# A diffusion step on one core: first modulation in four rounds, and low halves moved between engines

## The chip, the cores and the metric

The kernel runs on one core of one Trainium2 chip. The metric is the device time of the program in microseconds. Three runs of the kernel before took 1401.58, 1401.72 and 1401.97 us, median 1401.72. The program is bound by its order on one core; there is no traffic between cores.

## The reference

One inference step of a backbone with one trunk layer, for 128 context and 512 latent tokens of width 1024 (640 tokens in all, every weight shared, each kind of token with its own modulation vectors). Cut to what matters here:

```python
def trunk_layer(x, cond, ...):
    mod = (jax.nn.silu(cond) @ w_mod + b_mod)[:, None, :]          # 1024 -> 9 * 1024
    sh1, sc1, g1, sh2, sc2, g2, sh3, sc3, g3 = jnp.split(mod, N_MOD, axis=-1)
    h = rms_norm(x, norm_pre[0]) * (1.0 + sc1) + sh1
    x = x + 0.5 * g1 * rms_norm(swiglu(h, ffn_w_in[0], ffn_w_out[0]), norm_post[0])
    h = rms_norm(x, norm_pre[1]) * (1.0 + sc2) + sh2
    m, s_f, s_b = mixer(h, ...)                                    # Fourier mixing and HGRN2 scans
    x = x + g2 * rms_norm(m, norm_post[1])
    h = rms_norm(x, norm_pre[2]) * (1.0 + sc3) + sh3
    x = x + 0.5 * g3 * rms_norm(swiglu(h, ffn_w_in[1], ffn_w_out[1]), norm_post[2])
```

`swiglu(h, w_in, w_out)` is `(silu(h @ w_in[:, :2816]) * (h @ w_in[:, 2816:])) @ w_out`. Everything is float32.

## The kernel before, in words

**Precision.** Every large product is made of three TensorE passes over rounded operands: a float32 matrix is split into a high half (rounded to the fp32r format by ScalarE) and a low half (full minus high, by GpSimd or VectorE), and the passes are high x high, high x low, low x high. A slab is one block of weights (1024 x 128, 512 KB). Its life is: load (the queue of SyncE), high half on ScalarE (`next_hi`, L1211), low half on GpSimd in two instructions of 512 columns (`subtract`, L541) or on VectorE in one (`slab_low`, L1838, for the slabs listed in `LO_DVE`), and then the matmuls, after which `slab_done` frees its buffer.

**The order** is written out by hand, one list for each engine, with semaphores between them. `plan()` says for each slab which buffer it uses and after which slab it may be loaded.

**The start.** The tokens are normalized and transposed to features (XH). The first shift and scale vectors are `silu(cond)` times four blocks of 512 columns of `w_mod` (blocks 0 and 2 hold the first half of the features' shift and scale, 1 and 3 the second). `early_mod(i)` makes one block: 8 matmuls of 32 output rows (traced as 16, since float32 takes two instructions), four beside each other in the array. ScalarE copies the result (`mod_rows`, L1254), `fold_mod` (L685) turns it round into columns, VectorE adds the bias and forms the gains (L1745, L1755), then for each feature tile k the affine (`first_affine`, L1762, two instructions), ScalarE's high half (`first_hi`, L1258) and VectorE's low half (L1777). TensorE is kept busy by `keep_busy` in between. `first_slab(n, ks)` (L877) multiplies slab n with the feature tiles ks. The first three slabs are interleaved with the second round of the modulation; the low halves of slabs 1 and 2 on GpSimd wait until VectorE has finished tile 1 and tile 4 (`h0_ready`).

**The FFN's input product.** Of its 22 pairs of slabs (gate and value), three are made plainly; for the other 19 four blocks of the product are made with seven block products instead of eight (`seven_products`, L813 is `product`). They need combinations of the tokens (T1, T2, T4 as high and low halves, T3) and sums of weight blocks (S). `token_lows` has GpSimd make the low halves of T2, T1 and T4 in a row, 128 x 1280 each (L550); `seven_low` then makes those of each pair. The first product of the first pair writes the first bank of its set, the second the second bank, and so on.

**The FFN's output product** is `out0A` (token tiles 0 to 2) and then `out0B` (tiles 3 and 4), 22 slabs each, L630 to L632.

## Time and profile before

| | |
|---|---|
| median of three runs | 1401.72 us |
| the profiled execution | 1401.38 us |
| its span | 1399.2 us |
| TensorE matmul busy | 1376.1 us (98%) |
| VectorE busy | 745.8 us (53%) |
| ScalarE busy | 582.2 us (42%) |
| GpSimd busy | 727.0 us (52%) |
| granted TensorE clock, mean | 0.999 |
| DMA | 173.34 MB, mean 124 GB/s |

The span runs from the first to the last instruction; the profiled execution's time is 2.2 us longer. A granted clock of 1.00 is 2.4 GHz, 0.50 is 1.2 GHz. In the rows PE is TensorE's matmul, PEld its weight load, DVE VectorE, ACT ScalarE, POOL GpSimd. Matmuls are pipelined, so one matmul's duration is longer than the distance to the next.

### The profile page before, as it was taken

Reading aid. Unit: us, or ns where it says so; the run is one execution under the profiler, and the core shown is the slowest. Engines: PE = TensorE matmul, PEld = TensorE weight load, DVE = VectorE, ACT = ScalarE, POOL = GpSimd, SP = SyncE. Lnnn points to the kernel's source line nnn. Section 1 sums busy time; section 2 is a strip of 40 time slices with the busy share of each in tenths; the row PEclk is TensorE's granted clock in tenths of the full one; section 3 lists DMA queues with packets and bytes.
Section 4 is the critical chain, followed back from the end, with each engine's and each line's share of the span. In section 5 each row is a group of like instructions: output and inputs, shape, how many; then the busy total and the mean of one; then the engine's idle time right before and its main releaser. Section 6 shows DMA issues by size and latency. Waiting matters only on the chain.

```text
span 1399.2 us, 23472 instructions
## 1 busy us (share of the span) xinstructions
PE 1376.1 (98%) x9537; PEld 1258.3 (90%) x9537; DVE 745.8 (53%) x1109; ACT 582.2 (42%) x946; POOL 727.0 (52%) x530
## 2 busy tenths in 40 slices
PE   6999999999999999999999999999999999999998
PEld 5789898999887888999999999988999999998886
DVE  5686555766702421478776312135877666676033
ACT  5243333334534663244445222257344443455243
POOL 1475546465966672323223433542576555667663
PEclk9999999999999999999999999999999999999999
DMA  9756676233535651212112222333122223334465
GB/s 346 260 160 217 214 237 210 62 92 90 176 124 166 194 174 49 61 55 62 53 41 66 76 76 76 103 109 91 46 76 81 78 84 91 91 105 152 135 194 181
DMA packets 215294, 173.34 MB, mean 124 GB/s; under 512 B 6472, under 2 KB 175636, under 8 KB 215060
## 3 DMA queue, kind: packets, MB, share of 16 engines
q1 hardware_dynamic: 212448, 170.61, 39.0%
q8 instruction: 76, 1.25, 0.4%
q10 hardware_dynamic: 2740, 1.24, 0.3%
q14 instruction: 30, 0.25, 0.1%
HBM read 168.65 MB, written 3.17 MB: 123 GB/s over the span
## 4 chain that ended last, share of the span: by engine, by line
PE 89%; DVE 4%; DMA 2%; ACT 2%; POOL 2%; issue 1%; SPq 0%; DVEq 0%; ACTq 0%
PE PP L813 33%; PE PP L611 22%; PE PP L630 8%; PE PP L632 8%; PE PP L631 8%; PE PP L669 2%; DMA W_in<-in_ffn_w_in 1%; PE PP L877 1%; PE PP L655 1%; PE PP L1003 1%; POOL W_lo L541 1%; PE PP L1019 1%; POOL T_lo L550 0%; DVE XTOK L1802 0%; PE PP L1073 0%
## 5 line engine op out<-in xcount | busy, mean ns | idle before, releaser
L541 POOL TENSOR_TENSOR W_lo<-W_in,W_hi 128x512 fp32r<-128x512 f32 (+1 forms) x304 | 382.3, 1283 | 443.5 <-ACT W_hi L1211 436.1
L550 POOL TENSOR_TENSOR W_lo<-W_in,W_hi 128x512 fp32r<-128x512 f32 x112 | 176.3, 1587 | 185.1 <-ACT S_hi L1438 182.0
L1211 ACT ACTIVATE W_hi<-W_in 128x1024 fp32r<-128x1024 f32 x143 | 150.9, 1056 | 226.0 <-PE PP L632 115.8
L630 PE MATMUL PP<-W_hi,Mlo 128*128 128x512 f32 x440 | 172.0, 391 | 1.3 <-POOL W_lo L541 0.9
L632 PE MATMUL PP<-W_hi,Mhi 128*128 128x512 f32 x440 | 171.2, 389 | 0.0
L631 PE MATMUL PP<-W_lo,Mlo 128*128 128x512 f32 x440 | 171.2, 389 | 0.0
L611 PE MATMUL PP<-Hhi,W_hi 128*128 128x320 f32 (+2 forms) x608 | 146.6, 316 | 0.0
L813 PE MATMUL PP<-Hhi,W_hi 128*128 128x320 f32 x452 | 141.3, 313 | 1.3 <-POOL W_lo L550 0.9
L611 PE MATMUL PP<-Hlo,W_hi 128*128 128x320 f32 (+2 forms) x608 | 142.3, 309 | 0.0
L611 PE MATMUL PP<-Hhi,W_lo 128*128 128x320 f32 (+2 forms) x608 | 142.3, 309 | 0.0
L813 PE MATMUL PP<-Hhi,W_lo 128*128 128x320 f32 x452 | 139.6, 309 | 0.0
L813 PE MATMUL PP<-Hlo,W_hi 128*128 128x320 f32 x452 | 139.6, 309 | 0.0
L550 POOL TENSOR_TENSOR S_lo<-S_in,S_hi 128x512 fp32r<-128x512 f32 x76 | 116.4, 1531 | 0.0
L611 PEld LDWEIGHTS PP<-Hhi,W_hi 128*128 128x128 f32 x608 | 101.3, 188 | 3.9 <-issue 2.7
L611 PEld LDWEIGHTS PP<-Hhi,W_lo 128*128 128x128 f32 x608 | 102.7, 188 | 0.0
L611 PEld LDWEIGHTS PP<-Hlo,W_hi 128*128 128x128 f32 x608 | 102.7, 188 | 0.0
L630 PEld LDWEIGHTS PP<-W_hi,Mlo 128*128 128x128 f32 x440 | 82.6, 188 | 20.0 <-POOL W_lo L541 1.7
L632 PEld LDWEIGHTS PP<-W_hi,Mhi 128*128 128x128 f32 x440 | 82.6, 188 | 17.2
L631 PEld LDWEIGHTS PP<-W_lo,Mlo 128*128 128x128 f32 x440 | 82.6, 188 | 16.9
L813 PEld LDWEIGHTS PP<-Hhi,W_hi 128*128 128x128 f32 x452 | 84.8, 188 | 11.8 <-issue 9.1
L813 PE MATMUL PP<-T_hi,S_hi 128*128 128x320 f32 x304 | 94.0, 309 | 0.8 <-DVE M L2035 0.8
L813 PE MATMUL PP<-T_hi,S_lo 128*128 128x320 f32 x304 | 93.9, 309 | 0.0
(297 smaller groups left out, 3002.3 us busy)
## 6 DMA issues: line engine op xcount, KB each, us to landing
W_in<-in_ffn_w_out SPq DMA_DIRECT2D x176, 256.0 KB, 3.2
W_in<-in_ffn_w_in SPq DMA_DIRECT2D x84, 512.0 KB, 4.5
modl<-in_w_mod SPq DMA_DIRECT2D x14, 2048.0 KB, 7.9
W_in<-in_w_in SPq DMA_DIRECT2D x32, 512.0 KB, 3.8
modw<-in_w_mod SPq DMA_DIRECT2D x4, 2048.0 KB, 14.3
HL<-g_rows SPq DMA_DIRECT2D x6, 512.0 KB, 6.2
V_in<-in_w_in SPq DMA_DIRECT2D x10, 256.0 KB, 3.7
O_in<-in_w_out SPq DMA_DIRECT2D x10, 256.0 KB, 5.4
```

The lines of the kernel that those rows point to most:

```text
L541: return nc.gpsimd.tensor_tensor(lo[:, k0:k1, :], full[:, k0:k1, :], hi[:, k0:k1, :].bitcast(fp32), ALU.subtract)
L550: return nc.gpsimd.tensor_tensor(lo, full, hi.bitcast(fp32), ALU.subtract)
L611: m = mm(out[:, 0:c1 - c0], w[:, k, :], src[:, c0:c1], start=lead and n == 0 and a == 0, stop=tail and n == len(x) - 1 and a == 2)
L630: mm(out, xh, wh, start=lead and kk == 0, stop=False)
L631: mm(out, xh, wl, start=False, stop=False)
L632: m = mm(out, xl, wh, start=False, stop=tail and kk == 1)
L655: return nc.tensor.transpose(out, in_, ident[0:k, 0:k])
L669: m = mm(PP[3][32 * q:32 * q + 32, 0, :], S2[:, k, 30 - 2 * i:62 - 2 * i], w[:, k, :], start=first and k < 4, stop=k >= 4, skip_group_chec ...
L813: m = mm(out, wk[:, k, :], xk[:, k, :], start=not add and k == 0 and a == 0, stop=k == KH - 1 and a == 2, skip_group_check=add)
L877: m = mm(PP[n][:, half, 0:HALF], w[:, k, :], src[:, half * HALF:(half + 1) * HALF], start=k == 0 and a == 0, stop=k == KT - 1 and a == 2)
L1003: m = mm(near(pair_of(hd, lev))[32 * q:32 * q + 32, ch, :], KX[lev % 2][:, at:at + 32], queries, start=True, stop=True)
L1211: A(W[i][0], W[i][2], ACT.Copy).then_inc(hi_done, 1)
```

## The change

Four things are changed.

1. The first modulation is made in four rounds of 256 features (two tiles k) instead of two of 512. Each round loads 256 columns of the shift and 256 of the scale (`modw`, now eight buffers of 1 MB), makes them with matmuls of 256 columns, copies 256 columns and turns them with two matmuls instead of four. Loads, TensorE, ScalarE and VectorE are ordered by these rounds: slabs 0 and 1 are loaded behind the first round, slab 2 behind the second. ScalarE rounds slabs 0 and 1 before it copies the first row. `keep_busy` runs 32 times instead of 30.
2. GpSimd's low half of slab 2 waits for feature tile 2 instead of tile 4.
3. In both FFNs GpSimd's low half of T4 is made behind the low half of the first gate's slab. In the first pair of the first FFN the banks are 4, 5, 0, 3 instead of 4, 2, 0, 3, and the wait for the last of the three plain pairs stands before the third product instead of the second; the second pair gets two waits for the banks it shares.
4. In `out0B` VectorE makes the low half of slab 2 and GpSimd that of slab 3, instead of the other way round.

On TensorE, from the token transposes on, in the kernel before. `modw_162` to `modw_165` are the four blocks of 512 columns, `modw_164` to `modw_171` of the changed kernel the eight of 256; L669 and L679 are `mod_slab`, L685 and L696 `fold_mod`, L655 and L665 transposes, L877 and L895 `first_slab`.

```order
L655 MATMUL PP<-ident,YB 128x128 x40
L669 MATMUL PP<-modw_162,S_169 32x512 x8
L669 MATMUL PP<-modw_163,S_169 32x512 x8
L685 MATMUL PP<-ident,modrow_160 128x32 x4
L655 MATMUL PP<-ident 128x128 x30
L877 MATMUL PP<-Hhi,W_hi 128x320 x2
```

The same place in the changed kernel:

```order
L665 MATMUL PP<-ident,YB 128x128 x40
L679 MATMUL PP<-modw_164,S_175 32x256 x8
L679 MATMUL PP<-modw_165,S_175 32x256 x8
L696 MATMUL PP<-ident,modrow_160 128x32 x2
L665 MATMUL PP<-ident 128x128 x32
L895 MATMUL PP<-Hhi,W_hi 128x320 x2
L895 MATMUL PP<-Hlo,W_hi 128x320 x2
L895 MATMUL PP<-Hhi,W_lo 128x320 x2
L895 MATMUL PP<-Hhi,W_hi 128x320 x2
L895 MATMUL PP<-Hlo,W_hi 128x320 x2
L895 MATMUL PP<-Hhi,W_lo 128x320 x2
L679 MATMUL PP<-modw_166,S_175 32x256 x8
```

The second round's matmuls now stand behind two pieces of the first slabs, where eight pieces stood before the second round of 512 columns; the third and fourth follow between later pieces.

On GpSimd, where the seven-product stage of the first FFN begins, in the kernel before. W12 is the first gate's slab, W2 the first value's, S0 and S2 are sums of weight blocks.

```order
L550 TENSOR_TENSOR T2_lo_213<-T2_in_214,T2_hi_212 128x1280
L550 TENSOR_TENSOR T1_lo_216<-T1_in_217,T1_hi_215 128x1280
L550 TENSOR_TENSOR T4_lo_219<-T4_in_220,T4_hi_218 128x1280
L550 TENSOR_TENSOR W12_lo_141<-W12_in_142,W12_hi_140 128x512
L550 TENSOR_TENSOR S_lo0_144<-S_in0_145,S_hi0_143 128x512
```

The same place in the changed kernel:

```order
L557 TENSOR_TENSOR T2_lo_219<-T2_in_220,T2_hi_218 128x1280
L557 TENSOR_TENSOR T1_lo_222<-T1_in_223,T1_hi_221 128x1280
L557 TENSOR_TENSOR W12_lo_141<-W12_in_142,W12_hi_140 128x512
L557 TENSOR_TENSOR T4_lo_225<-T4_in_226,T4_hi_224 128x1280
L557 TENSOR_TENSOR S_lo0_144<-S_in0_145,S_hi0_143 128x512
```

The low half of T4 has gone behind that of the first gate. The diff, without line numbers' shifts, the placement of the new buffers and renamed counts:

```diff
--- before.py
+++ after.py
@@ -135,7 +136,7 @@
     BASE, BUF, FREE, ORDER, NEED, FRESH = plan()
 
     FIRST_LO = [(0, 0), (1, 0), (2, 0), (0, 1), (1, 1), (2, 1)]
-    LO_DVE = [BASE["out0B"] + m for m in (3, 7, 10, 13, 17)]
+    LO_DVE = [BASE["out0B"] + m for m in (2, 7, 10, 13, 17)]
     LO_DVE += [BASE["out1B"] + m for m in (3, 6, 9, 12, 15, 18, 20, 21)]
 
     top = [(nc.sbuf_base + 31) // 32 * 32]
...
@@ -380,6 +381,8 @@
 
     def seven_banks(f, p):
 
+        if (f, p) == (0, 0):
+            return [bank(n)[:, 0:HALF] for n in (4, 5, 0, 3)]
         sets = (((4, 2, 0, 3), (5, 2, 1, 3)), ((4, 5, 0, 1), (6, 7, 2, 3)))[f]
         return [bank(n)[:, 0:HALF] for n in sets[p % 2]]
 
...
@@ -407,8 +410,8 @@
 
         wm = w_mod[0].rearrange("(k p) n -> p k n", p=P)
         def load_early_mod(i):
-            n = MOD_ROUNDS[i // 2][i % 2]
-            sp.dma_start(modw[i][:, :, :], wm[:, :, n * 512:(n + 1) * 512]).then_inc(sem(f"modw_in{i}"), 16)
+            first_col = i % 2 * D + i // 2 * 256
+            sp.dma_start(modw[i][:, :, :], wm[:, :, first_col:first_col + 256]).then_inc(sem(f"modw_in{i}"), 16)
 
         def load(i, k0, kn, src):
 
...
@@ -460,17 +463,21 @@
 
         load_early_mod(0)
         load_early_mod(1)
-        for n in range(3):
-            load_in0(n)
+        load_in0(0)
+        load_in0(1)
         load_early_mod(2)
         load_early_mod(3)
+        load_in0(2)
+        for i in range(4, 7):
+            load_early_mod(i)
+        load_early_mod(7)
         load_in0(3)
         load_mod(0)
-        sp.wait_ge(sem("mod_mm"), MOD_EARLY)
+        sp.wait_ge(sem("mod_mm"), MOD_FIRST)
         load_mod(1)
         def next_mod(i):
 
-            sp.wait_ge(sem("mod_mm"), MOD_EARLY + (1 if i == 2 else i))
+            sp.wait_ge(sem("mod_mm"), MOD_FIRST + (1 if i == 2 else i))
             load_mod(i)
 
         for n in (4, 5):
...
@@ -544,13 +551,13 @@
         for i, half in FIRST_LO:
             pool.wait_ge(hi_done, i + 1)
             if half == 0 and i:
-                pool.wait_ge(sem("h0_ready"), (1, KT // 2)[i - 1])
+                pool.wait_ge(sem("h0_ready"), (1, 2)[i - 1])
             subtract(i, 4 * half, 4 * half + 4).then_inc(sem("first_lo"), 1)
         def low(hi, lo, full):
             return nc.gpsimd.tensor_tensor(lo, full, hi.bitcast(fp32), ALU.subtract)
 
         def token_lows(f):
-            for n, x in enumerate((T2, T1, T4)):
+            for n, x in enumerate((T2, T1)):
                 pool.wait_ge(sem("t_hi"), 3 * f + n + 1)
                 low(*(y[:, :, :] for y in x)).then_inc(sem("t_lo"), 1)
 
...
@@ -562,6 +569,9 @@
             pool.wait_ge(sem("s_made"), 4 * p + 3)
             pool.wait_ge(sem("seven_hi"), 7 * p + 1)
             low(*(x[:, 0:KH, :] for x in gate)).then_inc(sem("seven_lo"), 1)
+            if p == f * SEVEN:
+                pool.wait_ge(sem("t_hi"), 3 * f + 3)
+                low(*(y[:, :, :] for y in T4)).then_inc(sem("t_lo"), 1)
             pool.wait_ge(sem("seven_hi"), 7 * p + 4)
             low(*(x[:, :, :] for x in s1)).then_inc(sem("seven_lo"), 1)
             pool.wait_ge(sem("seven_hi"), 7 * p + 5)
...
@@ -661,27 +671,28 @@
         transpose(PP[2][:, 1, 0:36], rowsB[:, :]).then_inc(sem("vec_T"), 1)
         pe.wait_ge(sem("ones_set"), 2)
 
-        def mod_slab(w, i, first=False):
+        def mod_slab(w, i, first=False, cols=slice(0, 512)):
 
 
             for k in range(KT):
                 q = k % 4
-                m = mm(PP[3][32 * q:32 * q + 32, 0, :], S2[:, k, 30 - 2 * i:62 - 2 * i], w[:, k, :],
+                m = mm(PP[3][32 * q:32 * q + 32, 0, cols], S2[:, k, 30 - 2 * i:62 - 2 * i], w[:, k, :],
                        start=first and k < 4, stop=k >= 4, skip_group_check=not first)
             m.then_inc(sem("mod_mm"), 1)
 
         def early_mod(i):
             pe.wait_ge(sem(f"modw_in{i}"), 16)
             pe.wait_ge(sem("silu_c"), 2)
-            if i == 2:
-                pe.wait_ge(sem("modrow"), 1)
-            mod_slab(modw[i], i % 2, i % 2 == 0)
-
-        def fold_mod(i, rows):
+            r = i // 2
+            if r > 1:
+                pe.wait_ge(sem("modrow"), r - 1)
+            mod_slab(modw[i], i % 2, i % 2 == 0, slice(r % 2 * 256, r % 2 * 256 + 256))
+
+        def fold_mod(i, rows, first_at):
 
             pe.wait_ge(sem("modrow"), i + 1)
-            for q in range(4):
-                at = i * P + q * 32
+            for q in range(rows.shape[1] // P):
+                at = first_at + q * 32
                 m = mm(PP[3][:, 1, at:at + 32], rows[:, q * P:(q + 1) * P], ident[:, P:P + 32],
                        start=True, stop=True)
             m.then_inc(sem("mod_fold"), 1)
...
@@ -709,9 +720,9 @@
             first_tile(t)
         early_mod(0)
         early_mod(1)
-        fold_mod(0, modrow[0])
+        fold_mod(0, modrow[0], 0)
         pe.wait_ge(sem("x0_feat"), NCH)
-        keep_busy(30, PP[2][:, 1, 0:P])
+        keep_busy(32, PP[2][:, 1, 0:P])
 
 
         def to_features(b, t):
...
@@ -832,19 +843,26 @@
             pe.wait_ge(sem("seven_lo"), 5 * p + 1)
             if second and f:
                 pe.wait_ge(sem("hid_ready"), 3 * EARLY_PAIRS)
+            elif second:
+                pe.wait_ge(sem("u3_done"), 1)
             elif not first and not second:
                 pe.wait_ge(sem("hid_a"), p - 1)
             product(x, quadrant(gate, 0, KH), b11).then_inc(sem("product"), 1)
             pe.wait_ge(sem("seven_lo_dve"), 2 * p + 1)
             if first:
                 pe.wait_ge(sem("t_lo"), 3 * f + 1)
-                pe.wait_ge(sem("hid_ready"), (1 + f) * EARLY_PAIRS)
-            elif not (f and second):
+                if f:
+                    pe.wait_ge(sem("hid_ready"), 2 * EARLY_PAIRS)
+            elif second and not f:
+
+                pe.wait_ge(sem("hid_ready"), EARLY_PAIRS)
+            elif not second:
                 pe.wait_ge(sem("u3_done"), back)
             product(y, s2, T2).then_inc(sem("product"), 1)
             pe.wait_ge(sem("seven_lo"), 5 * p + 2)
             if first:
                 pe.wait_ge(sem("t_lo"), 3 * f + 2)
+                pe.wait_ge(sem("hid_ready"), (1 + f) * EARLY_PAIRS)
             elif not second:
                 pe.wait_ge(sem("hid_b"), p - 1)
             product(z, s1, T1).then_inc(sem("product"), 1)
...
@@ -893,16 +911,31 @@
             if n in MOD_AFTER:
                 late_mod(MOD_AFTER.index(n))
 
-        for k in range(KT // 2):
+        first_slab(0, (0,))
+        first_slab(1, (0,))
+        early_mod(2)
+        early_mod(3)
+        first_slab(0, (1,))
+        fold_mod(1, modrow[1], 64)
+        first_slab(1, (1,))
+        first_slab(2, (0, 1))
+        for k in (2, 3):
             first_slab(0, (k,))
             first_slab(1, (k,))
-        early_mod(2)
-        early_mod(3)
-        first_slab(2, (0,))
-        fold_mod(1, modrow[1])
-        first_slab(2, (1, 2, 3))
-        for n in range(3):
-            first_slab(n, range(KT // 2, KT))
+        early_mod(4)
+        early_mod(5)
+        first_slab(2, (2,))
+        fold_mod(2, modrow[2], 128)
+        first_slab(2, (3,))
+        early_mod(6)
+        early_mod(7)
+        first_slab(0, (4,))
+        fold_mod(3, modrow[3], 192)
+        first_slab(0, (5,))
+        first_slab(1, (4, 5))
+        first_slab(0, (6, 7))
+        first_slab(1, (6, 7))
+        first_slab(2, range(KT // 2, KT))
         late_mods(2)
         for j in range(1, EARLY_PAIRS):
             if j == 1:
...
@@ -1249,25 +1282,32 @@
         act.wait_ge(sem("lb_max"), 1)
         A(LB[:, 1:3, :], LB[:, 1:3, :], ACT.Exp).then_inc(sem("lb_exp"), 1)
 
-        def mod_rows(slabs, rows):
+        def mod_rows(slabs, rows, cols):
             act.wait_ge(sem("mod_mm"), slabs)
-            A(rows[:, :], PP[3][:, 0, :], ACT.Copy).then_inc(sem("modrow"), 1)
+            A(rows[:, :], PP[3][:, 0, cols], ACT.Copy).then_inc(sem("modrow"), 1)
+
+        def first_rows(r):
+            mod_rows(2 * r + 2, modrow[r], slice(r % 2 * 256, r % 2 * 256 + 256))
 
         def first_hi(k):
             act.wait_ge(sem("h0_32"), k + 1)
             A(Hhi[:, k, :], HL32[:, k, :], ACT.Copy).then_inc(sem("h0_hi"), 1)
 
         next_hi()
-        mod_rows(2, modrow[0])
         next_hi()
+        first_rows(0)
         first_hi(0)
         first_hi(1)
         next_hi()
+        first_rows(1)
         first_hi(2)
         first_hi(3)
-        mod_rows(MOD_EARLY, modrow[1])
-        for k in range(KT // 2, KT):
-            first_hi(k)
+        first_rows(2)
+        first_hi(4)
+        first_hi(5)
+        first_rows(3)
+        first_hi(6)
+        first_hi(7)
         next_hi()
 
 
...
@@ -1763,11 +1803,22 @@
                                     MV[:, k, cnd:cnd + 1], ALU.mult, ALU.add)
             m.then_inc(sem("h0_32"), 1)
 
+        def first_vectors(r):
+
+            def groups(ap):
+                step = ap.ap[1][0]
+                return bass.AP(ap.tensor, ap.offset, [ap.ap[0], [KT * step, 2], [step, 2]])
+
+            span = slice(2 * r, 2 * KT)
+            for cnd in range(2):
+                sums = PP[3][:, 1, 64 * r:64 * r + 64].rearrange("p (q i c) -> p i q c", q=2, c=2)
+                link(V.tensor_tensor(groups(MV[:, span, cnd]), sums[:, 0:2, :, cnd], groups(VA[:, span]), ALU.add))
+
         dve.wait_ge(sem("x0_feat"), NCH)
-        for r in range(2):
+        for r in range(ROUNDS):
             dve.wait_ge(sem("mod_fold"), r + 1)
-            mod_vectors(r * P, MOD_ROUNDS[r])
-            ks = range(r * KT // 2, (r + 1) * KT // 2)
+            first_vectors(r)
+            ks = range(2 * r, 2 * r + 2)
             gains(0, True, False, ks[0], ks[-1] + 1)
             first_affine(ks[0])
             for k in ks:
...
@@ -1841,7 +1892,7 @@
 
             for t in GROUP[0]:
                 y_gain(b, t, 0)
-            slab_low(OUT_B[b], 3)
+            slab_low(OUT_B[b], 3 if b else 2)
             for t in GROUP[0]:
                 y_gain(b, t, 1)
             if b == 0:
```

## Rows read from the trace of the kernel before

**Rows 1.** The page, part 1: busy time of TensorE, share of the span, instructions.

```profile
PE 1376.1 (98%) x9537; PEld 1258.3 (90%) x9537; DVE 745.8 (53%) x1109; ACT 582.2 (42%) x946; POOL 727.0 (52%) x530
```

**Rows 2.** TensorE's waits: who waited for whom: us, times, longest.

```profile
PE PP L877 <- DVE Hlo L1777: 1.3, 3, 0.7
PE PP L630 <- POOL W_lo L541: 0.9, 1, 0.9
PE PP L813 <- POOL W_lo L550: 0.9, 1, 0.9
PE PP L813 <- DVE M L2035: 0.8, 1, 0.8
```

**Rows 3.** Timeline of TensorE: start, duration, instructions merged [idle before them <- releaser].

```profile
21.32 1.92 PE L669 MATMUL PP<-modw,S 128*32 128x512 f32 x16 [0.71 <-DMA modw<-in_w_mod]
24.71 1.08 PE L685 MATMUL PP<-ident,modrow 128*128 128x32 f32 x8 [1.46 <-ACT modrow L1254]
25.62 5.14 PE L655 MATMUL PP<-ident 128*128 128x128 f32 x30
30.52 0.54 PE L877 MATMUL PP<-Hhi,W_hi 128*128 128x320 f32 x2
...
37.72 3.64 PE L669 MATMUL PP<-modw,S 128*32 128x512 f32 x32
...
42.28 0.97 PE L685 MATMUL PP<-ident,modrow 128*128 128x32 f32 x8
...
46.67 0.53 PE L877 MATMUL PP<-Hhi,W_hi 128*128 128x320 f32 x2 [0.70 <-DVE Hlo L1777]
...
58.49 1.92 PE L669 MATMUL PP<-modl,S 128*32 128x512 f32 x16
```

**Rows 4.** Stretches: length, busy time of each engine, granted clock, DMA share, GB/s.

```profile
14.00:16.00 2.00, 2.00 (x21) 2.00 (x20) 0.81 (x1) 1.98 (x3) 0.00 (x0) 1.00 1.06 389
...
22.00:23.00 1.00, 1.00 (x12) 0.13 (x4) 0.00 (x0) 0.00 (x0) 0.00 (x0) 1.00 1.20 290
...
28.00:29.00 1.00, 1.00 (x6) 1.00 (x5) 0.91 (x2) 1.00 (x3) 0.00 (x0) 0.50 1.06 391
```

**Rows 5.** Timelines of ScalarE, VectorE and GpSimd in the start.

```profile
24.08 0.58 ACT L1254 ACTIVATE modrow<-PP 128x512 f32<-128x512 f32 x1
...
29.05 1.79 DVE L1762 TENSOR_SCALAR HL<-XH,Avec,MV 128x128 f32<-128x128 f32 x2
...
46.44 0.80 DVE L1762 TENSOR_SCALAR HL<-XH,Avec,MV 128x128 f32<-128x128 f32 x2
...
29.28 1.28 POOL L541 TENSOR_TENSOR W_lo<-W_in,W_hi 128x512 fp32r<-128x512 f32 x1 [3.76 <-DVE Hlo L1777]
```

**Rows 6.** Timeline of TensorE's weight loads within one modulation block.

```profile
19.14 0.13 PEld L669 LDWEIGHTS PP<-modw,S 128*32 128x32 f32 x4 [0.30 <-issue]
```

**Rows 7.** Timelines of TensorE, VectorE, GpSimd at the first seven-product stage.

```profile
88.36 0.39 PE L813 MATMUL PP<-T_hi,S_hi 128*128 128x320 f32 x1 [0.79 <-DVE M L2035]
...
76.75 3.34 DVE L1929 TENSOR_TENSOR S_in<-S_in,W_in 128x512 f32<-128x512 f32 x1
...
73.19 9.73 POOL L550 TENSOR_TENSOR T_lo<-T_in,T_hi 128x1280 fp32r<-128x1280 f32 x3 [7.19 <-ACT T_hi L1450]
```

**Rows 8.** Timelines of TensorE, VectorE, ScalarE, GpSimd at the third slab of out0B.

```profile
441.55 0.50 PE L630 MATMUL PP<-W_hi,Mlo 128*128 128x512 f32 x1 [0.93 <-POOL W_lo L541]
...
439.13 1.23 DVE L1838 TENSOR_TENSOR W_lo<-W_in,W_hi 128x1024 fp32r<-128x1024 f32 x1 [44.81 <-ACT W_hi L1211]
...
436.83 2.27 ACT L1211 ACTIVATE W_hi<-W_in 128x1024 fp32r<-128x1024 f32 x2 [6.82 <-DMA W_in<-in_ffn_w_out]
...
437.97 3.52 POOL L541 TENSOR_TENSOR W_lo<-W_in,W_hi 128x512 fp32r<-128x512 f32 x2 [4.75 <-ACT W_hi L1211]
```

**Rows 9.** Timelines of VectorE and GpSimd at the second seven-product stage.

```profile
1001.57 3.45 DVE L1930 TENSOR_TENSOR I_in<-W_in,I_in 128x512 f32<-128x512 f32 x1
...
997.89 9.95 POOL L550 TENSOR_TENSOR T_lo<-T_in,T_hi 128x1280 fp32r<-128x1280 f32 x3 [13.97 <-ACT T_hi L1450]
1007.80 1.72 POOL L550 TENSOR_TENSOR W_lo<-W_in,W_hi 128x512 fp32r<-128x512 f32 x1
```

More of the change, by code:

```diff
@@ L61 @@
 ]
-MOD_ROUNDS = ((0, 2), (1, 3))
+ROUNDS = 4
+MOD_FIRST = 2 * ROUNDS
 MOD_AFTER = [2, 3, 5]
@@ L225, in hybrid_step_kernel @@
     rowsB = place("rowsB", [36, P], fp32, at=tile_at(8) + 512)
-    modrow = [place(f"modrow{r}", [P, 512], fp32, at=tile_at(8) + 1024 + 2048 * r) for r in range(2)]
+    modrow = [place(f"modrow{r}", [P, 256], fp32, at=tile_at(8) + 1024 + 1024 * r) for r in range(ROUNDS)]
     late_at = [tile_at(MOD_LATE_FREE), tile_at(FT + MOD_LATE_FREE)]
     early_at = late_at[0] + 16384 + 2 * 2048
-    modw = [place(f"modw{s}", [P, KT, 512], fp32, at=at)
-            for s, at in enumerate((h_at + KT * TB, early_at, early_at + 16384, early_at + 2 * 16384))]
+    modw = [place(f"modw{s}", [P, KT, 256], fp32, at=at + s % 2 * 8192) for s, at in enumerate(
+        at for at in (h_at + KT * TB, early_at, early_at + 16384, early_at + 2 * 16384) for _ in range(2))]
     modl = [place(f"modl{s}", [P, KT, 512], fp32, at=late_at[s]) for s in (0, 1)]
@@ L480, in _ @@
         load(BASE["in0s"] + 1, 0, KT, w0[:, :, DFF + j * P:DFF + (j + 1) * P])
-        sp.wait_ge(sem("mod_mm"), MOD_EARLY + 2)
+        sp.wait_ge(sem("mod_mm"), MOD_FIRST + 2)
         load(BASE["in0s"], 0, KT, w0[:, :, j * P:(j + 1) * P])
@@ L887, in late_mod @@
             if i == 0:
-                pe.wait_ge(sem("modrow"), 2)
+                pe.wait_ge(sem("modrow"), ROUNDS)
             mod_slab(modl[int(i == 1)], i, i == 0)
@@ L927, in _ @@
             if p == last_mod + 1:
-                fold_mod(2, modrowl)
+                fold_mod(ROUNDS, modrowl, 2 * P)
             if p == last_mod + 3:
@@ L1418, in late_rows @@
             if p == last_mod + 1:
-                mod_rows(MOD_EARLY + MOD_LATE, modrowl)
+                mod_rows(MOD_FIRST + MOD_LATE, modrowl, slice(0, 512))
             if p == last_mod + 4:
@@ L1974, in late_vectors @@
         def late_vectors():
-            dve.wait_ge(sem("mod_fold"), 3)
+            dve.wait_ge(sem("mod_fold"), ROUNDS + 1)
             mod_vectors(2 * P, range(MOD_EARLY, MOD_EARLY + MOD_LATE))
```

## The prediction

> **What bounds the kernel now.** I read the page first: TensorE is busy 1376 of 1399 us [rows 1], and the clock row is full almost throughout. So only TensorE's own work, and the stretches in which it stands still or does filler, can change the time. The second view is the list of TensorE's waits [rows 2]: beside the first small loads, which the change leaves alone, there are four short ones, 1.3 + 0.9 + 0.9 + 0.8 us. The third is the timeline at each of them. All other engines matter only through what they deliver there.
>
> The first 58.5 us are laid out in [rows 3]. The first half of the modulation is waited for until 21.3 us (a load), its result is turned round from 24.7 to 25.7, 30 filler transposes run to 30.5, then the first three slabs run in pieces of one slab by one k tile (six matmuls). Eight pieces fill 30.52 to 37.72, so one is 0.88 us and starting again after a stop costs some 0.15. The second half of the modulation stands at 37.72 (two slabs, 3.6 us). The first FFN's next stage starts at 58.49.
>
> **The start, load by load.** A 1 KB row is in no trace of before. [rows 4] give its neighbours: rows of 2 KB move at 389 GB/s (14:16), rows of 512 B at 290 (22:23). A cost per row plus a cost per byte through the two makes 1 KB rows 348 GB/s; the bounds are 291 and 387. Before, the two 2.1 MB loads landed at 21.3 [rows 3], so at 387 GB/s they began at 10.5. Two quarter loads (2.1 MB together) now land at 10.5 + 6.0 = 16.5, before TensorE is free for them at 18.7. Slabs 0 and 1 (0.52 MB each, 1.8 us) land at 18.3 and 20.1, the next two quarters at 26.1, slab 2 at 27.9, the last quarter 4.2 MB later at 39.9. ScalarE now rounds slab 1 ahead of the modulation row: 20.1 + 1.06, then a copy of 0.4 us (0.58 for twice the columns [rows 5]), so the turning starts at 21.6 instead of 24.71: 3.1 us earlier.
>
> The Trainium skill (DMA: Bandwidth & Descriptors, Specifications) puts the line rate at transfers of 512 B and more. The trace disagrees, 290 against 389 GB/s. By that rule the quarters would cost nothing extra, slab 2 would land 1.2 us sooner, and this would be the third rival below.
>
> **The modulation matmuls.** In four rounds of 256 columns the same columns are computed, but three of four rounds now lie behind the first real matmul instead of one of two. Does half the width cost half? The weight loads come four together and then wait 0.30 us, one group per 0.43 us [rows 6]: the time is the columns', not the weight load's. So a slab of 256 columns should be 4 x 0.21, and two of them 1.85 us with the restart, where two of 512 are 3.64. The upper bound is 3.6 for such a pair, no saving at all. I take 1.85, since the burst shows room. Behind the start: three pairs 5.6 instead of 3.6 (+2.0), three turnings of half the size, 3 x 0.45 instead of 0.8 (+0.5). So 2.5 of the 3.1 us go into moved work.
>
> **The chain inside the start.** A turning is followed by VectorE vectors, affine, ScalarE rounding, VectorE low. Before, from the start of the turning at 42.28 to the first matmul that used it at 46.67 is 4.4 us [rows 3], and with half the turning 4.0. That chain now occurs three times behind the start. Round 1: whether the filler (32 transposes) runs at 2.4 GHz, 2.8 us, or as before mostly at 1.2 GHz, the granted clock of 0.50 at 28:29 [rows 4] with 4.9 us, the first slab begins between 25.5 (its low half's time) and 27.4; two pieces, a modulation pair and one piece later the turning starts at 30.4 to 31.9, and its k tile is due at 34.4 to 35.9. But GpSimd is let go for slab 2 at 29.0, when ScalarE has rounded it, and has four low halves of 1.28 us in a row, to 34.1. While one such ran at 29.28, a pair of VectorE affines took 1.79 us instead of 0.80 [rows 5]. In the early case VectorE meets two of them, +2.0, in the late one half of one: 36.4 either way. TensorE runs out of pieces at 33.5 to 35.0 and stands 1.4 to 2.9 us. From there the path is fixed: four pieces 3.5, pair 1.85, one piece, turning at 42.6, k tile 4 at 46.6 (TensorE, with a piece and a pair, is there at 45.9: 0.7 idle), a piece, turning at 47.5, k tile 6 at 51.5 (0.7 idle after four pieces), eight pieces 7.0: end at 58.5. Before it was 58.49. The start yields 0.0, with bounds of -1.8 (GpSimd not in the way) and +2 (below).
>
> The Trainium skill (SBUF — State Buffer, SBUF: two separate sides) says that the port shared by VectorE and GpSimd is an exclusive lock for a whole instruction. The trace agrees: 3.34 us for an add of 512 columns beside GpSimd's 9.73 us triple [rows 7]. By this rule the meeting above is met in full, as in the sum; without it the start would end near 56.7.
>
> **Where the first FFN's seven-product stage begins.** TensorE waits 0.79 us at 88.36 for the third hidden tile, made late by VectorE, whose additions took 3.3 to 3.4 us each beside GpSimd's three token lows, 73.19 to 82.92 [rows 7]. They start when the load of 69.6 lands, which TensorE's own progress releases, so this whole group moves with it. After: the second product writes bank 5, which is free, and the wait for the hidden tile stands before the third product, 1.76 us (twelve matmuls) later. The third token low goes behind the gate's low. VectorE is free of GpSimd sooner, but meets the moved low at its second weight low, and I find the tile at 87.6 (now 88.2); it is then due at 89.1. The queue behind the moved low on GpSimd is the S low (88.0, due 89.1) and the value lows (90.1, due 90.9). All is covered; the wait goes, -0.95 with its restart. If that cover were 1 us short, nothing would be left.
>
> **The second output block.** TensorE waits 0.93 us to 441.55, 1.09 with the restart, so from 440.46, for the low of slab 2: ScalarE begins to round it at 436.83 and is done by 437.9, GpSimd only at 441.49 [rows 8]. VectorE, idle until its low for slab 3 at 439.13 (1.23 us), now takes slab 2, to 439.2; due 440.46. GpSimd gets slab 3, rounded at 439.1, two halves, to 441.7 or at most 442.6 by the 3.5 us that it took beside VectorE; due 443.2. VectorE's next work starts no later than now. -1.1.
>
> **The third place, second FFN.** TensorE waits 0.9 us [rows 2] for the gate's low, which queues behind three token lows and runs 1007.80 to 1009.52 [rows 9]. Two token lows (9.95 us for three before) end at 1004.5; the low waits for VectorE's third sum (1005.0 [rows 9]) and is done at 1006.8, before TensorE's 1008.6. -1.0. Behind it: third token low to 1010.1, S low 1011.9 (due 1012.2), first value low 1014.0 (due 1013.95), second 1016.1 (due 1017.5). So 0 to 0.3 may come back. I take -0.95.
>
> **Sum.** 0.0 - 0.95 - 1.1 - 0.95 = -3.0 us. Everything between these places is TensorE's own work and its loads are released by it, so the shift passes through. The profiled execution took 1401.38 us (span 1399.2 and 2.2 around it), so 1398.4 on its terms; the median of the three runs is 0.34 above it: 1398.7.
>
> **Rivals.**
> A, the clock falls in the start. It fell at 26.6 after a stretch with two idle pieces (20.4 to 21.3, 23.1 to 24.7), and was at 0.50 at 28:29 and back at 30, some 3.4 us [rows 3, 4]. The idle 1.4 to 2.9 us at 34 could do the same; half speed for 3.4 us costs 1.7: -1.3, 1400.4. Against it: shorter in all. 0.18.
> B, slower: a modulation slab of 256 columns costs as much as one of 512 (a fixed cost of a group of four). Six slabs by 0.92 is +5.5: -3.0 + 5.5 = +2.5, or with a clock loss +4.2, 1404 to 1406. It decides against the change from 0.5 us extra per slab. For it: no such width is in the trace; against it, the 0.30 us in which weight loads wait [rows 6]. 0.05.
> C, slab 2 lands at 26.7 or VectorE's affines are held up less: the start gives -1.3 to -1.8, 1397.2. 0.22.
> D, the reordering doesn't do what it says at one of the two seven-product places (GpSimd's later lows are the new wait): 1 us comes back, 1399.7. 0.12.
> The forecast has the remaining 0.43.
>
> A measurement of this kernel tells about 0.2% (2.8 us) from no change, so the boundary is 1398.9. The forecast, 1398.7 +- 0.7, is a little more often than not below it (0.25 of its 0.43); C is below; a part of D and A with a better start (0.05) too: faster 0.52. Slower, above 1404.5, is B with a little: 0.05. The rest, 0.43, is same. The range from C's best to A with D's loss on top: 1396.5 to 1401.3.
>
> **What would show it.** Modulation rows of TensorE of 32 matmuls in about 1.9 us (B: 3.6). First real matmul between 25 and 28. The first matmul of k tile 2 at 36 to 37, with GpSimd's four lows ending near 34 (C: at 35). A granted clock of 1.00 from 30 to 60 (A: 0.50 somewhere). Start of the late modulation slab near 58.5. No waits of 0.8 to 0.9 us near 88, 441 and 1008. I am wrong if the start is off by more than 1.5 us, or if one of the three waits stays.

## The result, and the profile after

| | time, median (range) | profiled execution | its span |
|---|---|---|---|
| before | 1401.45 us (1400.19 to 1402.26, 15 runs) | 1401.38 | 1399.2 |
| changed | 1403.97 us (1401.98 to 1407.26, 15 runs) | 1403.97 | 1401.7 |

The ratio is 1.0019 (1.0012 to 1.0026): 2.5 us slower, where 1398.7 was forecast, and above the range's upper end of 1401.3. The first part of the page answers to [rows 1]: TensorE is 1.2 us busier, and 66 instructions more.

```profile
PE 1377.3 (98%) x9603; PEld 1260.8 (90%) x9603; DVE 748.7 (53%) x1117; ACT 582.6 (42%) x948; POOL 725.7 (52%) x530
```

The start of the changed kernel, TensorE's timeline (start, duration, instructions merged, [idle before them <- releaser]), to be laid beside [rows 3]:

```profile
19.10 1.93 PE L679 MATMUL PP<-modw,S 128*32 128x256 f32 x32
21.91 0.63 PE L696 MATMUL PP<-ident,modrow 128*128 128x32 f32 x4 [0.87 <-ACT modrow L1287]
22.37 3.69 PE L665 MATMUL PP<-ident 128*128 128x128 f32 x32
26.01 0.53 PE L895 MATMUL PP<-Hhi,W_hi 128*128 128x320 f32 x2
...
31.71 0.53 PE L696 MATMUL PP<-ident,modrow 128*128 128x32 f32 x4
...
34.50 0.46 PE L895 MATMUL PP<-Hhi,W_lo 128*128 128x320 f32 x2
37.66 0.87 PE L895 MATMUL PP<-Hhi,W_hi 128*128 128x320 f32 x2 [2.70 <-DVE Hlo L1828]
38.33 0.73 PE L895 MATMUL PP<-Hlo,W_hi 128*128 128x320 f32 x2
...
40.99 0.46 PE L895 MATMUL PP<-Hhi,W_hi 128*128 128x320 f32 x2
...
49.62 0.54 PE L895 MATMUL PP<-Hhi,W_hi 128*128 128x320 f32 x2 [0.58 <-DVE Hlo L1828]
...
54.51 0.53 PE L895 MATMUL PP<-Hhi,W_hi 128*128 128x320 f32 x2 [0.69 <-DVE Hlo L1828]
...
61.71 1.92 PE L679 MATMUL PP<-modl,S 128*32 128x512 f32 x16
```

The late modulation slab begins at 61.71 instead of 58.49: the start alone costs 3.2 us. TensorE stands 2.70 us before the first matmul of k tile 2, and the matmuls behind it show 0.73 us a pair instead of 0.46 (they start 0.53 us apart instead of 0.29). The stretches there (length, busy time of TensorE, its weight loads, VectorE, ScalarE, GpSimd, granted clock, DMA share, GB/s) show the clock at its lower level:

```profile
37.00:38.00 1.00, 0.34 (x1) 0.38 (x2) 1.00 (x2) 0.36 (x1) 0.00 (x0) 0.79 1.11 349
38.00:39.00 1.00, 1.00 (x5) 1.00 (x5) 0.24 (x1) 0.00 (x0) 0.00 (x0) 0.50 1.10 346
...
41.00:42.00 1.00, 1.00 (x8) 1.00 (x8) 0.00 (x0) 0.00 (x0) 0.00 (x0) 1.00 1.07 355
```

The 349 GB/s is the rate of 1 KB rows, for which the prediction had 348. What made k tile 2 late stands on ScalarE, GpSimd and VectorE. Slab 2 landed at 29.19 (forecast 27.9), so that GpSimd's four lows end at 35.34 (forecast 34.1). VectorE's gains (1.45 us) lie wholly beside them, its affines (2.44 us, from 34.15) for the first 1.2 us:

```profile
29.19 1.06 ACT L1244 ACTIVATE W_hi<-W_in 128x1024 fp32r<-128x1024 f32 x1 [3.47 <-DMA W_in<-in_ffn_w_in]
...
30.32 5.02 POOL L548 TENSOR_TENSOR W_lo<-W_in,W_hi 128x512 fp32r<-128x512 f32 x4 [2.59 <-ACT W_hi L1244]
...
32.67 1.45 DVE L1795 SCALAR_TENSOR_TENSOR Avec<-MV,VA 128x2 f32<-128x2 f32 x2
34.15 2.44 DVE L1802 TENSOR_SCALAR HL<-XH,Avec,MV 128x128 f32<-128x128 f32 x4
...
46.65 0.36 DVE L1795 SCALAR_TENSOR_TENSOR Avec<-MV,VA 128x2 f32<-128x2 f32 x2
47.04 1.52 DVE L1802 TENSOR_SCALAR HL<-XH,Avec,MV 128x128 f32<-128x128 f32 x4
```

One round later, with GpSimd idle, the same work takes 0.36 and 1.52. The three stops that the reorderings aimed at, 88.36, 441.55 and 1009.58 ([rows 2, 7, 8]), are gone. Others are there: TensorE's rows of the changed kernel

```profile
381.41 0.50 PE L640 MATMUL PP<-W_hi,Mlo 128*128 128x512 f32 x1 [1.13 <-DVE Mhi L2022]
...
1015.91 0.41 PE L824 MATMUL PP<-Hhi,I_hi 128*128 128x320 f32 x1 [0.41 <-POOL I_lo L557]
...
1349.65 0.50 PE L640 MATMUL PP<-W_hi,Mlo 128*128 128x512 f32 x1 [0.50 <-POOL W_lo L548]
```

To compare kernels, I cut every trace at seven matmuls of TensorE: the late modulation slab (A), the stop near 276 on VectorE's TT (B), the stop near 465 in the first FFN's second output block (C), the first attention matmul near 589 (D), the first of the second FFN's seven products (E), the first matmul of its output stage (F), the last row (G). A is a time, the rest are the lengths of the stretches between, each the difference of two starts, in us:

| kernel | A | A-B | B-C | C-D | D-E | E-F | F-G |
|---|---|---|---|---|---|---|---|
| before | 58.49 | 217.65 | 188.67 | 124.39 | 420.38 | 234.18 | 149.50 |
| before, second profile (y_again) | 58.55 | 217.67 | 189.02 | 124.36 | 419.98 | 234.18 | 149.59 |
| changed | 61.71 | 216.63 | 188.90 | 124.36 | 418.45 | 235.13 | 150.64 |
| changed, second profile (x_again) | 62.16 | 216.64 | 188.68 | 124.35 | 418.76 | 235.12 | 150.06 |
| a_junctions | 57.99 | 216.63 | 188.12 | 124.34 | 419.74 | 235.02 | 149.43 |
| b_rounds | 61.36 | 217.66 | 188.46 | 124.34 | 419.41 | 234.28 | 150.98 |
| d_slab2 | 57.78 | 216.64 | 188.22 | 124.35 | 418.45 | 235.13 | 150.87 |
| e_hold | 57.72 | 216.63 | 188.77 | 124.34 | 418.73 | 235.11 | 150.87 |
| c3_filler | 60.67 | 216.63 | 188.66 | 124.32 | 418.46 | 235.11 | 150.00 |
| g_value | 58.49 | 216.64 | 189.19 | 124.36 | 419.35 | 235.05 | 149.43 |
| f_swap | 58.51 | 217.66 | 188.13 | 124.34 | 419.95 | 234.18 | 149.48 |
| h_first | 57.97 | 216.63 | 189.16 | 124.37 | 420.20 | 234.18 | 149.61 |
| i_third | 58.43 | 217.68 | 188.58 | 124.36 | 419.82 | 235.02 | 149.77 |
| k_split | 58.10 | 216.63 | 188.94 | 124.36 | 418.89 | 235.02 | 149.71 |

Changed against before: +3.22 - 1.02 + 0.23 - 0.03 - 1.93 + 0.95 + 1.14 = +2.56 us.

### The profile page after: what moved, and what is told of

It is laid out like the page before. It is cut to its first block, busy times and chain, and to the rows that moved or that the text cites. A ratio compares the mean times of both kernels' runs of the same rounds, so it can differ in the third digit from the quotient of the medians.

```text
span 1401.7 us, 23627 instructions
## 1 busy us (share of the span) xinstructions
PE 1377.3 (98%) x9603; PEld 1260.8 (90%) x9603; DVE 748.7 (53%) x1117; ACT 582.6 (42%) x948; POOL 725.7 (52%) x530
## 4 chain that ended last, share of the span: by engine, by line
PE 92%; DVE 3%; DMA 1%; POOL 1%; ACT 1%; SPq 1%; issue 1%; DVEq 0%; ACTq 0%; POOLq 0%
PE PP L824 33%; PE PP L621 24%; PE PP L640 9%; PE PP L642 9%; PE PP L641 9%; PE PP L679 2%; PE PP L895 1%; PE PP L1036 1%; PE PP L665 1%; DMA W_in<-in_ffn_w_out 1%; DMA W_in<-in_ffn_w_in 1%; PE PP L1052 1%; POOL W_lo L548 1%; PE PP L1106 0%; PE PP L660 0%
## 5 line engine op out<-in xcount | busy, mean ns | idle before, releaser
L824 PE MATMUL PP<-T_lo,S_hi 128*128 128x320 f32 x304 | 93.9, 309 | 0.0
```

What stands on the lines that cost most here:

```text
L824: m = mm(out, wk[:, k, :], xk[:, k, :], start=not add and k == 0 and a == 0, stop=k == KH - 1 and a == 2, skip_group_check=add)
```

## Experiments

Every time is a median beside runs of the kernel before on the same chip.

**a_junctions and b_rounds: the change in two.** The first is the kernel before with the change's hunks in `LO_DVE`, `seven_banks`, `token_lows`, `seven_low`, `seven_products` and the call of `slab_low`; the second is the kernel before with all the other hunks. Two lines on which they differ (- is b, + is a):

```diff
-ROUNDS = 4
+MOD_ROUNDS = ((0, 2), (1, 3))
...
-            for n, x in enumerate((T2, T1, T4)):
+            for n, x in enumerate((T2, T1)):
```

> The modulation in two rounds as before, with only the three reordered places (third token low behind the first gate's low, bank 5 for the second product, slab 2's low on VectorE in the second output block). Theory: these three gain and the start alone loses; the waits of 0.8, 0.9 and 0.9 us near 88, 441 and 1009 go, 0.4 comes back at 1015: -2.4 to -3.0 us against before, about 1398.7. Rival: what they gain comes back behind them, as the new waits of 1.1 us at 381 and 0.5 us at 1350 in the changed kernel suggest: then they yield -0.5 to -1.4 and those two waits are seen here too.

> The modulation in four rounds alone, the three places as before. Theory: the start costs all of the loss and hides a gain: +4.5 to +5.5 us against before (1406), the late modulation slab near 61.7 instead of 58.5, and the three waits near 91, 443 and 1011 back. Rival (the loss lies behind the start): +0 to +1.5.

Measured: a 1399.29 us (before 1401.21; ratio 0.9990, 0.9981 to 0.9999), 1.9 us faster. b 1404.7 (ratio 1.0029, 1.0018 to 1.0040). Both lie between what I expected and its rival. So the four rounds lose 3.5 us and the reorderings win 1.9, not 3.0. (g_value and k_split below, which have the three reorderings and two rounds as well, are 1.5 and 2.5 under their runs of before: the three can't be told apart.) In b the same stop stands in the start (2.67 us at 37.34), A is 61.36.

**d_slab2: the load of slab 2 ahead of the second round's loads.**

```diff
         load_in0(1)
+        load_in0(2)
         load_early_mod(2)
         load_early_mod(3)
-        load_in0(2)
```

> The changed kernel with the load of slab 2 ahead of the second round's two modulation loads. Theory: slab 2 lands near 23 instead of 29.2, GpSimd's four lows run from 26.6 (behind the second feature tile) or 27.7 to 32.8 and are out of VectorE's way; the second round's loads land at 28, before TensorE asks for them at 28.9. The first piece of feature tile 2 starts at 35.7 instead of 37.7 and the stop is 1.4 instead of 2.7 us: -2.0, and -3.5 if the clock then doesn't fall, so 1400.5 to 1402. Rival (VectorE's chain isn't held up by GpSimd): the piece still starts at 37 or later and nothing changes.

Measured: 1400.51 us (ratio 0.9993, 0.9984 to 1.0002), 3.5 us under the changed kernel. ScalarE has slab 2 at 25.24 and GpSimd's lows end at 32.3. VectorE's gains, from 32.27, take 0.35 us and its affines 1.51:

```profile
25.62 6.69 POOL L548 TENSOR_TENSOR W_lo<-W_in,W_hi 128x512 fp32r<-128x512 f32 x5 [4.82 <-DVE Hlo L1828]
...
57.78 1.93 PE L679 MATMUL PP<-modl,S 128*32 128x512 f32 x16
```

The stop before k tile 2 is 0.69 us (at 35.25), and the clock stays full.

**e_hold: slab 2 as late as in the changed kernel, but GpSimd out of the way.** d moves the load and the lows together. Here the load stays late:

```diff
                 pool.wait_ge(sem("h0_ready"), (1, 2)[i - 1])
+            if (i, half) == (0, 1):
+                pool.wait_ge(sem("h0_ready"), 4)
             subtract(i, 4 * half, 4 * half + 4).then_inc(sem("first_lo"), 1)
```

> The changed kernel with its load order, but GpSimd, when it has done the first half of slab 2 (30.3 to 31.6), waits for k tile 3 of the first hidden input before it takes the three second halves, so that nothing of GpSimd's runs beside VectorE's affines of k tile 2. Theory (slab 2 is late only in that GpSimd's burst then meets VectorE): VectorE's two gains take 0.36 instead of 1.45 and its four affines 1.52 instead of 2.44, the first matmul of k tile 2 comes at 35.2 to 35.6 instead of 37.66, TensorE stands 0.4 to 0.8 us, the clock stays full, the late modulation slab begins at 57.8 and the time is 1400.0 to 1400.8. Rival (the slab's own lateness holds TensorE, or GpSimd's put-off halves are late for k tile 4): a wait of over 1.5 us stays near 35, or a wait for a low half comes near 46, and the time is 1402 to 1404.

Measured: 1400.46 us (ratio 0.9993, 0.9984 to 1.0002). GpSimd, VectorE and TensorE of this kernel:

```profile
30.20 1.28 POOL L548 TENSOR_TENSOR W_lo<-W_in,W_hi 128x512 fp32r<-128x512 f32 x1 [2.94 <-ACT W_hi L1246]
35.89 3.80 POOL L548 TENSOR_TENSOR W_lo<-W_in,W_hi 128x512 fp32r<-128x512 f32 x3 [4.41 <-DVE Hlo L1830]
...
32.19 0.36 DVE L1797 SCALAR_TENSOR_TENSOR Avec<-MV,VA 128x2 f32<-128x2 f32 x2
32.58 1.51 DVE L1804 TENSOR_SCALAR HL<-XH,Avec,MV 128x128 f32<-128x128 f32 x4
...
31.23 0.53 PE L698 MATMUL PP<-ident,modrow 128*128 128x32 f32 x4
...
35.16 0.53 PE L897 MATMUL PP<-Hhi,W_hi 128*128 128x320 f32 x2 [0.69 <-DVE Hlo L1830]
...
57.72 1.92 PE L681 MATMUL PP<-modl,S 128*32 128x512 f32 x16
```

The slab is as late as before, and A is still 57.72. Its lateness costs nothing by itself; it costs by where it puts GpSimd's burst. Of the 3.99 us between the two kernels' A, 0.48 was there before the place of the edit: this profile's second turning began at 31.23, that of the changed kernel at 31.71. From the turning to the first matmul of k tile 2 it is 3.93 us for 5.95 (2.02 less), and from there to A 22.56 for 24.05 (1.49 less, the clock). The one wait on GpSimd is worth these 3.5 us.

**c3_filler: the stop kept, but filled.** 30 filler transposes between the last piece of k tile 1 and the first of k tile 2:

```diff
         first_slab(2, (0, 1))
+        keep_busy(30, PP[3][:, 0, 3 * P:4 * P])
```

> The changed kernel with 30 filler transposes (0.087 us each, 2.6 us) in the place where TensorE stands still for 2.7 us before the first matmul of k tile 2 (34.96 to 37.66 in the changed kernel); nothing is made ready earlier. Theory (the half speed of 37.7 to 41 is the price of that standing still): the first matmul of k tile 2 stays at 37.6 to 37.8, but the matmuls behind it take 0.46 us a pair instead of 0.73, the granted clock stays at 1.00 from 37 to 41, the late modulation slab begins at 60.2 instead of 61.7, and the time is about 1402.5, 1.5 us under the changed kernel's 1404.0. Rival (the clock falls for another reason, or the 1.5 us are the wait's): the granted clock still shows 0.50 and the time is 1404 or more.

Measured: 1401.84 us (ratio 1.0003, 0.9994 to 1.0012), 2.1 under the changed kernel. TensorE's timeline, then one stretch:

```profile
34.92 3.44 PE L665 MATMUL PP<-ident 128*128 128x128 f32 x30
38.11 0.54 PE L895 MATMUL PP<-Hhi,W_hi 128*128 128x320 f32 x2
38.49 0.46 PE L895 MATMUL PP<-Hlo,W_hi 128*128 128x320 f32 x2
```

```profile
38.00:39.00 1.00, 1.00 (x10) 1.00 (x9) 0.45 (x1) 0.00 (x0) 0.00 (x0) 1.00 1.10 351
```

The first piece comes 0.45 us later, and A 1.04 earlier (60.67): from that piece to A it is 22.56 us, as in e_hold (57.72 - 35.16), against 24.05 in the changed kernel. The half clock is worth 1.5 us, and it comes from the standing still. Of the 2.1 us in the time, only that 1.04 lies in the start; the rest lies in later stretches (F-G is 150.00 for 150.64), which the filler doesn't touch.

**x_again and y_again: each kernel's profile a second time.**

> The changed kernel once more, unaltered, one look. Its first profile shows two waits that the kernel before has not, 1.13 us at 381.41 and 0.50 us at 1349.65, both behind a slab load that landed late. If these belong to the change, they come again at the same size (within 0.1 us); if they come from how long the small loads ahead of the slab's in SyncE's queue happen to take, they come at another size or not at all. The 2.7 us stand at 37.66 and the half clock behind it should come again as they are.

> The kernel before once more, unaltered, one look. If the stop at 441.55 (1.09 us) belongs to the order of the lows, it comes again at its size. If it depends on when the slab loads land, it is another size or gone, with a stop near 378 in its place, and the stretch from 276.1 to 464.8 still takes 188 to 189 us.

Measured, one execution each: 1403.91 and 1401.47 us. The stand before k tile 2 and the half clock came again (2.99 us at 38.07). The stops behind loads came at other sizes: 0.88 for 1.13 at 381, 0.28 at 1341 for 0.50 at 1349, and 0.74 for 0.93 at 441 in the kernel before. The stop near 380 also stands in a kernel with two rounds, where its row reads

```profile
378.12 0.50 PE L638 MATMUL PP<-W_hi,Mlo 128*128 128x512 f32 x1 [1.02 <-DVE Mhi L1986]
```

(g_value). So it doesn't need the four rounds. But g_value has the three reorderings, so this doesn't free the change of it: a stop of 0.23 us or more stands there in nine of the ten profiles with four rounds or with the first reordering, and in none of the four with neither. In the changed kernel ScalarE waited for that slab's load, which SyncE issues behind two of gain rows (512 KB each) and the mask's (448 KB):

```profile
366.13 1.89 SPq L449 DMA_DIRECT2D YB<-in_t_mask  x1
368.07 13.16 SPq L428 DMA_DIRECT2D W_in<-in_ffn_w_out  x8
...
376.41 1.06 ACT L1244 ACTIVATE W_hi<-W_in 128x1024 fp32r<-128x1024 f32 x1 [5.82 <-DMA W_in<-in_ffn_w_out]
```

The mask's load held the queue for 1.89 us here and for 3.06 in b_rounds and 3.14 in x_again. It varies, but the stops are not its size (the longest stop stands beside the shortest of the three). It goes out 87.8 to 88.0 us behind B in thirteen of the fourteen profiles (88.7 in y_again), so TensorE's progress does release it. What differs is when the slab behind it lands: ScalarE takes it up 98.07 us behind B in the changed kernel, 97.14 in h_first (stop 0.23), 96.92 in f_swap (no stop), and in every profile with such a stop its length is, within 0.03 us, what that start is over 96.94. What makes the load land late, and whether it comes with the change, is open.

**h_first, f_swap, i_third: one reordering each, in the kernel before.** h_first has the bank, the moved wait and the first FFN's moved token low. The other two:

```diff
-    LO_DVE = [BASE["out0B"] + m for m in (3, 7, 10, 13, 17)]
+    LO_DVE = [BASE["out0B"] + m for m in (2, 7, 10, 13, 17)]
-            slab_low(OUT_B[b], 3)
+            slab_low(OUT_B[b], 3 if b else 2)
...
-            for n, x in enumerate((T2, T1, T4)):
+            for n, x in enumerate((T2, T1) if f else (T2, T1, T4)):
+            if f and p == SEVEN:
+                pool.wait_ge(sem("t_hi"), 6)
+                low(*(y[:, :, :] for y in T4)).then_inc(sem("t_lo"), 1)
```

> The kernel before with the first FFN's seven-product edits alone (second product in a free bank, the wait for the third hidden tile ahead of the third product, the third token low behind the gate's low). Both the prediction and my theory: the stop of 0.79 us at 88.36 goes, and from the late modulation slab at 58.49 to the matmul of 276.14 it takes 216.6 instead of 217.65 us; time 1.0 us less, 1400.4. Rival: as at the other places something later takes the 1.0 us back by 276: 217.4 or more, 1401.2 or more.

> The kernel before with one edit: in the first FFN's second output block VectorE takes the low of slab 2 and GpSimd that of slab 3. The prediction's term: the stop of 1.09 us at 441.55 goes and its start passes through to the end, -1.1 (1400.3, with before at 1401.4). Theory now (this stretch is held by its slab loads, not by one low half): from the seven-product stage's start at 276 to the matmul of 464.8 it takes 188.1 to 189.0 us as before's 188.67, because a stop taken away at 441 stands a little earlier or later (near 378), and the time is 1401.4 +- 0.5.

> The kernel before with the second FFN's edit alone: the third token low behind the gate's low. The prediction's term: -0.95. Theory now: the stop at 1009.58 goes (1.1 with the restart), but a stop of 0.66 comes at the fourth product and one of 0.27 at the seventh, so that from the start of the first of the seven products to the next output stage (1009.58 to 1243.76 in the kernel before, 234.18 us) it takes 235.0 to 235.1: -0.2 in all, 1401.2.

Measured against 1401.46 for the kernel before: h_first 1400.28 (0.9983 to 1.0001), f_swap 1400.28 (0.9981 to 0.9999), i_third 1401.13 (0.9987 to 1.0004). The times alone hardly part them; the table does.
- First place: A-B is 216.63 or 216.64 in all nine profiles with it and 217.65 to 217.68 in the five profiles without: -1.02 (forecast -0.95).
- Second place: my expectation, no gain, was wrong in this run. B-C is 188.13 and the time 1.2 us less. Over all profiles it depends on the stop near 378. Where that is missing, B-C is 188.12 and 188.13 with the swap and 188.58, 188.67 and 189.02 without: 0.6 us. Where it is 0.7 us or more, B-C is 188.66 to 189.19 with the swap and 188.46 (b_rounds) without: nothing won, and b_rounds has no stop at 441 in the old order. That rests on b_rounds alone. d_slab2 (0.40 us, 188.22) and h_first (0.23 us, 189.16, old order) go with the first kind.
- Third place: the stop at 1009.58 goes, and E-F is 0.84 longer (235.02 for 234.18). D-E + E-F is 654.84 in i_third, 654.56 and 654.16 in the two profiles of before. Nothing is left.

**g_value: the third token low later still, behind the first value low, in the second FFN.**

> The kernel before with the three reorderings (two rounds), and in the second FFN GpSimd takes the third token low behind the first value low instead of ahead of the slab sum's low. Theory: the wait of 0.41 us at 1012.7 for the first value low goes, the second value low comes 0 to 0.3 us late for the sixth product, so 0.1 to 0.4 us under the run with the three reorderings alone (1399.3): 1398.9 to 1399.2. Rival: the moved low meets VectorE at a place where its sums are due, and a wait of 0.4 us or more comes between 1014 and 1022: no gain or a loss of up to 0.5, 1399.3 to 1399.8.

Measured: 1399.82 us (ratio 0.9986, 0.9978 to 0.9995), 0.5 above a_junctions, which is within what these runs can tell. The stop of 0.41 went, and another came at the seventh product:

```profile
1009.61 4.25 POOL L552 TENSOR_TENSOR T_lo<-T_in,T_hi 128x1280 fp32r<-128x1280 f32 x1
...
1012.22 2.20 DVE L1940 TENSOR_TENSOR S_in<-W_in 128x512 f32<-128x512 f32 x1
...
1019.49 0.39 PE L821 MATMUL PP<-Hhi,S_hi 128*128 128x320 f32 x1 [0.73 <-DVE TT L2025]
```

E-F is 235.05, as before this edit. The rival held: in both places that were tried, the long low gives the stop back further on.

**k_split: four more loads.** All six profiles with four rounds have F-G of 150.0 to 151.0, all those with two rounds 149.4 to 149.8; D-E is shorter with four. Here the two-round kernel issues each first modulation load as two halves of four k tiles:

```diff
-            sp.dma_start(modw[i][:, :, :], wm[:, :, n * 512:(n + 1) * 512]).then_inc(sem(f"modw_in{i}"), 16)
+            for k0 in (0, KT // 2):
+                sp.dma_start(modw[i][:, k0:k0 + KT // 2, :], wm[:, k0:k0 + KT // 2, n * 512:(n + 1) * 512])\
+                    .then_inc(sem(f"modw_in{i}"), 16)
```

> The kernel before with the three reorderings, where each of the four first modulation loads goes out as two (four k tiles each), rows of 2 KB as they were. In all profiles of kernels with four rounds (eight such loads instead of four) the last output stage, from its first matmul near 1243 to TensorE's last row, takes 150.0 to 151.0 us, in all with two rounds 149.4 to 149.8; between 589 and the second FFN's seven products it is the other way round (418.5 to 418.7 against 419.4 to 419.8 with the gate's wait gone). Theory (the number of loads issued before shifts how later loads fall): this kernel shows 150.0 to 151.0 and about 418.6, and a time of 1399.3 +- 0.7. Rival (it is something else of the four rounds): 149.4 to 149.8 and 419.3 to 419.8, at the same time.

Measured: 1399.54 us (ratio 0.9982, 0.9973 to 0.9991), F-G 149.71. The number of loads is not the cause, and my theory fell. The place can be told: in five of the six four-round profiles one or two stops behind GpSimd's lows of slabs stand between 1341 and 1351, 0.28 to 0.50 us each (the row at 1349.65 above is one), and none of 0.2 us or more stands behind F in the eight with two rounds. The sixth, c3_filler, has none there and the shortest F-G of the six. Why these lows come late stays open. D-E is 418.89, between the two groups, and tells nothing.

## Why the prediction was wrong, by its own steps

**The start (forecast 0.0, measured +3.2).** The earlier turning (21.91), the halved modulation pairs (1.93 us, forecast 1.85) and the rate of 1 KB rows were right, and so was the mechanism that delays k tile 2. What failed:
- Slab 2 landed 1.3 us later than forecast (29.19 for 27.9). 0.4 of it was there at slab 1 (ScalarE begins on it at 20.52, forecast 20.1). For the other 0.9 I had let the loads follow one another; slab 2's 512 B rows and the next quarter's 1 KB rows probably moved side by side (between 20.5 and 29.2 the DMA moved 2.9 MB, and two quarters and a slab are 2.6), but no run separates this.
- GpSimd's burst was to cost VectorE half of one low, 0.5 us; it cost 2.02 (e_hold: 3.93 us from the turning to k tile 2 for 5.95, with the slab equally late). Not all of that is the slab's lateness. The turning came at 31.71, within the forecast's 30.4 to 31.9, and VectorE's gains follow 0.96 us behind it, at 32.67, so even lows that ended at 34.1 would have lain beside them for 1.4 us. The sum priced the affines and left out the gains, which took 1.45 for 0.36. An estimate from these rows: with the slab on time the gains' 1.1 us would have stayed and the affines' 0.9 gone, the first matmul of k tile 2 at 36.7, a stop of 1.8 us. It came at 37.66 instead of 36.4: +1.3.
- The clock (rival A, chance 0.18) fell: +1.5, shown by c3_filler. I argued "shorter in all", from the stop's length before against this one's. The stop of 2.70 us lies at the long end of the forecast's 1.4 to 2.9, and it is that long because of the same meeting (0.69 in e_hold, without it): the later the slab, the longer the stop, and with the stop the clock. The two are not separate risks. Whether a stop of 1.4 us would have brought the clock down no run shows.
- The path from there was 22.56 us at full clock, not 22.1: +0.45.

Sum 1.3 + 1.5 + 0.45 = 3.25, against 3.22 measured. Rival C (slab 2 earlier, -1.3 to -1.8) gives 57.78 (d_slab2), -0.7: even then four rounds win only 0.2 to 0.8 us over the 57.97 to 58.55 of two rounds.

**First place (-0.95): right**, -1.02 in every profile.

**Second place (-1.1): the size was off**, 0.6 at best and nothing where TensorE was held near 378. The row of ScalarE that I used [rows 8] says "6.82 <-DMA W_in": that slab was waited for from a load, and I treated the stretch as TensorE's own. The step "its loads are released by it, so the shift passes through" failed in its second half: the loads are issued at the same distance behind B, but ScalarE takes up the slab between 96.58 and 98.07 us behind B, 1.5 us apart from profile to profile.

**Third place (-0.95): the stop went, and 0.84 of it came back.** I had the first value low 0 to 0.3 us late, and took none. It cost 0.66 with the restart. The seventh product came another 0.27 late; that VectorE, held beside GpSimd, made it so is read from the rows below, not tested. GpSimd and VectorE of the changed kernel:

```profile
1006.59 1.69 POOL L557 TENSOR_TENSOR W_lo<-W_in,W_hi 128x512 fp32r<-128x512 f32 x1 [0.63 <-DVE I_in L1981]
1008.23 3.42 POOL L557 TENSOR_TENSOR T_lo<-T_in,T_hi 128x1280 fp32r<-128x1280 f32 x1
1011.61 1.74 POOL L557 TENSOR_TENSOR S_lo<-S_in,S_hi 128x512 fp32r<-128x512 f32 x1
1013.32 4.23 POOL L557 TENSOR_TENSOR I_lo<-I_in,I_hi 128x512 fp32r<-128x512 f32 x2
...
1012.45 2.25 DVE L2035 TENSOR_TENSOR Hlo<-T_in,Hhi 128x1280 fp32r<-128x1280 f32 x1
```

This was rival D (0.12), and it should have been the forecast: the sum itself had the low 0.05 us late, and a stop of any length costs its restart too.

**The rest (forecast 0).** Four rounds make D-E some 0.9 us shorter (mean of 418.45 to 418.76 against that of 418.89 to 419.82, with the gate's stop gone in both) and F-G 1.0 longer, which nearly cancels. It was not foreseen. F-G's part stands in the stops behind GpSimd's lows near 1341 to 1351; what makes them, and D-E's part, is not explained.
